# A causal depthwise convolution moved from VectorE to banded products on TensorE, inside the attention stage of a hybrid decoder step

## The chip, the cores and the metric

The kernel runs on one core of one Trainium2 chip. The metric is the device time of one execution, in microseconds; the time shown is the median of three executions.

## The reference, cut to what matters

One inference step of one layer: 2064 prompt rows (16 meta tokens and 2048 tokens) and 8 sample rows with 512 cached positions each. One projection gives the operands of two branches. The convolution branch is a GLU, a causal depthwise convolution of width 31 over 512 channels, a LayerNorm over channels and a swish. The attention branch selects 256 keys a query (128 for the samples) and attends over them.

```python
u = ua * jax.nn.sigmoid(ub)
u_ext = jnp.pad(u, ((0, 0), (CONV_W - 1, 0), (0, 0)))          # samples: 30 rows of state_conv, then u
y = depthwise_conv(u_ext, w) + b                               # [T, 512], width 31
mu = jnp.mean(y, -1); var = jnp.mean((y - mu) ** 2, -1)
cy = silu((y - mu) * rsqrt(var + LN_EPS) * ln_g + ln_b)
o = sparse_attend(q, iq, iw, qpos, k, v, ik, rel_bias, topk)   # 8 heads of 64, 2 kv heads, T5 bias
x = x + concat([cy * silu(gc), o * silu(ga)]) @ w_out
```

## The kernel before, in words

Four functions follow each other, each with one instruction stream per engine and semaphores between them. `project_norm_and_keys` normalises x and makes keys and values. `project_and_select` makes the other projections in chunks of 128 columns by three blocks of up to three tiles of 128 tokens, and between the chunks scores the keys (TensorE and ScalarE) and searches for the selection threshold (VectorE). `attend_and_convolve` does attention and convolution. `mix_out` does the LayerNorm of the convolution, gates, the output projection and the last norm.

`attend_and_convolve` begins with a head: keys are transposed to `kh`, `kl`; 32 pages of K and 32 of V are loaded for the samples (`load_pages`, one DMA each with an address read from a table); the samples' attention runs (`S`, `sS`, then products with `vpage`, line 1387). A table `rrow` of relative biases is computed, written 128 times to DRAM (`d_r`) and read back skewed as `band` and `band16`. GpSimd adds band and mask to `bm`.

Then it takes 65 steps p over `pairs`: step 0 is the 16 rows of the last tile, steps 1 to 64 are the tiles 15 down to 0, four steps a tile, two heads a step. In step p TensorE computes the logits of step p+1 into `psU` (two buffers of 1024 columns, lines 1415 and 1416), VectorE adds mask or band and takes the row maximum (line 1292), ScalarE exponentiates (line 1167), and TensorE transposes the result of step p into `psT` (line 1423), ScalarE copies it to `pts` (line 1136) and TensorE multiplies it with V into `psO` (line 1439). The order on every engine is the program order of its loop; nothing is scheduled at run time.

The convolution is on VectorE: 8 units (4 channel groups by 2 halves of the tokens), each 31 taps of 1088 columns (`conv_tap`, lines 1236 and 1238). `dtaps` spreads these 248 instructions over the steps, behind the eviction of the logits of each step.

SyncE issues nearly all DMAs, in program order, with waits in between (`load_tile`, `load_u`). In `mix_out` the statistics of the LayerNorm are products with a matrix of ones (lines 1823 and 1830), with square, square root, reciprocal and two wide tensor operations per block of four tiles, and the weights are split into a high and a low part in eight pieces (ScalarE line 1663, GpSimd line 1634). TensorE's first product of the output projection (line 1810) waits for all eight.

## Time and profile before

| | |
|---|---|
| median of 3 runs | 2011.85 us (2005.34 to 2012.64) |
| profiled execution | 2016.47 us, its span 2014.5 us |
| busy, share of the span | TensorE 76%, VectorE 70%, ScalarE 36%, GpSimd 19% |
| DMA | 169675 packets, 164.60 MB, queue q1 27.2% of 16 engines |

Rows of the profile give times in microseconds from the start of the span. An engine's idle time in front of an instruction stands in square brackets, with what ended it. PE is TensorE's matmul, PEld its weight load, DVE is VectorE, ACT ScalarE, POOL GpSimd, SPq the issues of SyncE. A matmul on float32 operands makes two records, a transpose or a matmul on float32r operands one.

### The profile page before, as it was taken

Reading aid. Unit: us, or ns where it says so; the run is one execution under the profiler, and the core shown is the slowest. Engines: PE = TensorE matmul, PEld = TensorE weight load, DVE = VectorE, ACT = ScalarE, POOL = GpSimd, SP = SyncE. Lnnn points to the kernel's source line nnn. Section 1 sums busy time; section 2 is a strip of 40 time slices with the busy share of each in tenths; the row PEclk is TensorE's granted clock in tenths of the full one; section 3 lists DMA queues with packets and bytes.
Section 4 is the critical chain, followed back from the end, with each engine's and each line's share of the span. In section 5 each row is a group of like instructions: output and inputs, shape, how many; then the busy total and the mean of one; then the engine's idle time right before and its main releaser. Section 6 shows DMA issues by size and latency. Waiting matters only on the chain. (4 is left out here: it accounts for less than half of the span.)

```text
span 2014.5 us, 26783 instructions
## 1 busy us (share of the span) xinstructions
PE 1529.6 (76%) x9511; PEld 1284.5 (64%) x9511; DVE 1405.1 (70%) x2411; ACT 717.9 (36%) x1255; POOL 379.3 (19%) x265
## 2 busy tenths in 40 slices
PE   5879998399379659692445888888878777359998
PEld 5776997299269659591234666665556555237777
DVE  3414998898888898885018999888789997134442
ACT  3525321322143122221103554555445553254431
POOL 2120432044214114240000000000000112142211
PEclk9989999699689879796657999999899986579999
DMA  7631522023166112221350010111101111522332
GB/s 238 202 87 27 115 79 58 31 75 89 54 215 138 54 52 72 58 68 54 87 128 31 23 53 30 52 46 35 50 27 49 61 47 54 174 90 84 137 140 105
DMA packets 169675, 164.60 MB, mean 82 GB/s; under 512 B 54602, under 2 KB 141618, under 8 KB 169535
## 3 DMA queue, kind: packets, MB, share of 16 engines
q1 hardware_dynamic: 167239, 161.85, 27.2%
q8 instruction: 75, 1.23, 0.3%
q10 hardware_dynamic: 2304, 1.05, 0.2%
q14 instruction: 57, 0.47, 0.1%
HBM read 100.94 MB, written 57.93 MB: 79 GB/s over the span
## 5 line engine op out<-in xcount | busy, mean ns | idle before, releaser
L1238 DVE SCALAR_TENSOR_TENSOR cy<-cu,cw,cy 128x1088 f32<-128x1088 f32 x240 | 345.4, 1439 | 16.3 <-issue 1.3
L645 PE MATMUL psum<-xh,wh 128*128 128x384 f32 (+1 forms) x1056 | 346.4, 328 | 12.4 <-POOL wl L533 10.7
L645 PE MATMUL psum<-xh,wl 128*128 128x384 f32 (+1 forms) x1056 | 345.7, 327 | 0.0
L645 PE MATMUL psum<-xl,wh 128*128 128x384 f32 (+1 forms) x1056 | 345.6, 327 | 0.0
L1136 ACT ACTIVATE pts<-psT 128x512 f32<-128x512 f32 (+1 forms) x302 | 168.5, 573 | 293.3 <-PE psT L1423 282.8
L1415 PE MATMUL psU<-kh,qt 128*128 128x512 f32 (+3 forms) x320 | 139.6, 437 | 98.2 <-DVE mx L1292 96.0
L645 PEld LDWEIGHTS psum<-xh,wh 128*128 128x128 f32 x1056 | 199.0, 188 | 14.1 <-POOL wl L533 10.9
L1439 PE MATMUL psO<-pts,vs 128*64 128x128 f32 x2176 | 187.5, 295 | 23.0 <-ACT pts L1136 22.7
L645 PEld LDWEIGHTS psum<-xl,wh 128*128 128x128 f32 x1056 | 199.2, 189 | 0.0
L645 PEld LDWEIGHTS psum<-xh,wl 128*128 128x128 f32 x1056 | 199.2, 189 | 0.0
L1423 PE MATMUL psT<-cst,L 128*128 128x128 f32 x1105 | 186.8, 303 | 8.7 <-ACT L L1167 8.5
L761 DVE TENSOR_SCALAR_CACHE_REDUCE hit<-scores,T 128x2064 bf16<-128x2064 f32 (+14 forms) x120 | 184.6, 1538 | 11.0
L655 PE MATMUL psum<-ikh,iqs 128*128 128x512 f32 (+4 forms) x172 | 73.0, 427 | 149.3 <-ACT r L610 149.1
L1292 DVE CUSTOM_DVE_ANT_0 L<-psU,mask 128x1024 f32<-128x1024 f32 (+7 forms) x162 | 136.1, 861 | 68.1 <-PE psU L1416 31.1
L1167 ACT ACTIVATE L<-L,nm 128x1920 f32<-128x1920 f32 (+16 forms) x129 | 154.4, 1201 | 72.8 <-DVE nm L1297 72.4
L533 POOL TENSOR_TENSOR wl<-wst,wh 128x1024 fp32r<-128x1024 f32 x44 | 108.3, 2463 | 348.3 <-ACT wh L563 348.3
L1125 POOL TENSOR_TENSOR bm<-band,mask 128x2048 f32<-128x2048 f32 (+1 forms) x16 | 68.0, 4247 | 554.7 <-DMA mask<-d_mask 554.5
L1439 PEld LDWEIGHTS psO<-pts,vs 128*64 128x64 f32 x2176 | 118.7, 141 | 79.6 <-ACT pts L1136 54.2
L1423 PEld LDWEIGHTS psT<-cst,L 128*128 128x128 f32 x1105 | 132.6, 152 | 47.5 <-issue 22.1
L1415 PEld LDWEIGHTS psU<-kh,qt 128*128 128x128 f32 x320 | 67.8, 212 | 130.9 <-DVE mx L1292 95.6
L655 PEld LDWEIGHTS psum<-ikh,iqs 128*128 128x128 f32 x172 | 36.4, 212 | 166.0 <-ACT r L610 160.0
L610 ACT ACTIVATE r<-psum 128x1024 f32<-128x1024 f32 (+6 forms) x100 | 76.8, 807 | 174.5 <-DVE scores L708 143.7
(269 smaller groups left out, 2581.1 us busy)
## 6 DMA issues: line engine op xcount, KB each, us to landing
wst<-in_w_in SPq DMA_DIRECT2D x28, 512.0 KB
wst<-in_w_in SPq DMA_DIRECT2D x32, 256.0 KB
qt<-d_q SPq DMA_DIRECT2D x16, 512.0 KB, 4.2
xst<-in_x_prompt SPq DMA_DIRECT2D x15, 512.0 KB, 3.9
xr<-in_x_prompt SPq DMA_DIRECT2D x15, 512.0 KB, 4.3
out_y_prompt<-fin SPq DMA_DIRECT2D x15, 512.0 KB, 3.0
gate<-d_ga SPq DMA_DIRECT2D x17, 256.0 KB, 4.5
d_mix<-mix SPq DMA_DIRECT2D x17, 256.0 KB, 2.2
```

What stands on the lines that cost most here:

```text
L533: nc.gpsimd.tensor_tensor(out=wl[:, n % 2], in0=wst[:, n % 2], in1=wh[:, n % 2].bitcast(f32), op=ALU.subtract).then_inc(w_lo, 1)
L610: nc.scalar.activation(r[:, m % 2, 0:job[4]], u[:, 0:job[4]], ACT.Relu).then_inc(act_job, 1)
L645: last = nc.tensor.matmul(u[:, 0:k * P], a[:, w % 2, cc, :], x[:, s0:s0 + k, cc, :], start=(cc == 0 and e == 0), stop=(cc == KC - 1 and e ...
L655: nc.tensor.matmul(u[:, b0:b0 + bn], q, mem.ikh[:, a + b0:a + b0 + bn], start=True, stop=False)
L761: V.tensor_scalar(hit[:, 0:width(i)], scores[:, c, 0:width(i)], at[:, c:c + 1] if len(at.shape) == 2 else at[:, c], 0.0, ALU.is_ge, ALU.ad ...
L1136: A.activation(out, src, ACT.Copy).then_inc(act_pt, 1)
L1167: A.activation(L[:, b, 0:width(i)], L[:, b, 0:width(i)], ACT.Exp, bias=nm[:, b:b + 1], accum_out=es[:, tile_no[i] % 2, j % GRP + 4 * side: ...
L1238: V.scalar_tensor_tensor(y, u[:, k:k + HALFW], w, y, ALU.mult, ALU.add)
L1292: last = V.tensor_tensor_reduce(out=L[:, b, x0:x1], in0=U[:, job % 2, x0 - a:x1 - a], in1=in1, scale=1.0, scalar=3 * NEG, op0=ALU.add, op1 ...
L1415: T.matmul(u[:, b0:b0 + bn], q, kh[:, side, a + b0:a + b0 + bn], start=True, stop=False)
L1423: last = T.transpose(pt[:, (side * k + e) * P:(side * k + e + 1) * P], L[:, (2 * p + side) % 4, (b + e) * P:(b + e + 1) * P], ident)
L1439: last = T.matmul(OT[64 * side:64 * side + 64, tile_no[i] % 2, j * P:(j + 1) * P], vs[0:rows, b + e, 64 * side:64 * side + 64], pts[0:rows ...
```

## The change

The depthwise convolution becomes products with banded weight matrices. The tokens are cut into 65 windows of 32 outputs, with 62 input rows each, and 8 more windows hold the samples. For one channel, the weights `ht` are a band of 62 by 32 and the moving operand `uw` is 62 rows by 73 windows, so 512 channels are 512 matmuls, four of them in the four column groups of the array. For that `project_and_select` transposes the GLU output on TensorE (24 jobs `uT`, 68 transposes) and writes it token-major to `d_un`; conv weights go to `d_cw` with zeros around. In attention the channels are taken in four quarters (`load_windows`, `convolve`, `store_conv`), at the ends of steps 1 to 3, 6 to 8, 11 to 13 and 16 to 18. The outputs go to `d_yn` token-major; every second step from 23 on, one tile is loaded as rows, normalised on VectorE (`bn_stats`) and GpSimd (power), transposed by TensorE (`rows_to_columns`) and written to `d_y`. `mix_out` loses the LayerNorm, its weight pieces are split right behind block 0, and the samples' convolution is gone from it.

The head of attention: `rrow` is computed in `project_norm_and_keys` and `d_r` written in `project_and_select`. The page loads are split: SyncE issues 16 of K and 16 of V, GpSimd the others (before, ScalarE issued 16 of K, SyncE the rest). The samples' attention is cut in two on TensorE: the logits of step 0 stand between its scores and its products with V.

```diff
@@ constants
+WIN = 32
+WROWS = WIN + TAPS - 1
+NWP = -(-LP // WIN)
+NW = NWP + NS
@@ project_and_select
+                if name == "ua":
+                    late.append(("uT", h, j, b))
...
+                elif job[0] == "uT":
+                    pe.wait_ge(combined, m + 1)
+                    for e in range(slots(job[1], job[3])[1]):
+                        last = nc.tensor.transpose(u[:, e * P:(e + 1) * P], ust[:, m % 2, e * P:(e + 1) * P], ident)
...
+                if (h, c) == (0, 4):
+                    sp.dma_start(t.d_r.rearrange("t h x -> h t x"), mem.rrow[:, :].unsqueeze(1).to_broadcast([NH, P, BANDX])).then_inc(r_out, 16)
@@ attend_and_convolve
+NQ, QA = 4, 32
+BANKA = 512 // NW
+CONV_JOBS = [(q, a, min(BANKA, QA - a)) for q in range(NQ) for a in range(0, QA, BANKA)]
+CONV_STEPS = [(1, 2, 2, 3, 3), (6, 7, 7, 8, 8), (11, 12, 12, 13, 13), (16, 17, 17, 18, 18)]
+NORM_STEP = [23 + 2 * n for n in range(NT)]
...
+            def load_windows(q):
+                if q:
+                    sp.wait_ge(pe_pt, last_conv(q - 1))
+                else:
+                    sp.wait_ge(uw_zero, 1)
+                for r in range(2):
+                    c0 = 2 * P // 2 * q + 2 * QA * r
+                    at = slice(64 * r, 64 * r + WROWS)
+                    sp.dma_start(ht[at, :, :], bass.AP(t.d_cw.tensor, c0, [[C, WROWS], [C, WIN], [1, 2 * QA]])).then_inc(ht_in, 16)
+                    sp.dma_start(uw[at, 0:NWP, :], bass.AP(t.d_un.tensor, (UROW0 - TAPS + 1) * C + c0,
+                                                           [[C, WROWS], [WIN * C, NWP], [1, 2 * QA]])).then_inc(uw_in, 16)
...
+            def store_conv(q):
+                sp.wait_ge(act_pt, last_conv(q))
+                for g in range(4):
+                    sp.dma_start(bass.AP(t.d_yn.tensor, c0, [[C, WIN], [WIN * C, NWP], [1, QA]]),
+                                 yc[WIN * g:WIN * g + WIN, q % 2, 0:NWP, :]).then_inc(yc_out[q % 2], 16)
...
-            load_pages(sp, range(half), ptab, t.cache_k, "o s n d -> (o s) (n d)", kpage, pg_in)
-            load_pages(sp, range(NS * NPAGE), ptab, t.cache_v, "o s n d -> (o s) (n d)", vpage, vp_in)
+            load_pages(sp, range(hp), ptab, t.cache_k, "o s n d -> (o s) (n d)", kpage, pg_in)
             load_tile(0)
-            sp.wait_ge(rrow_done, 1)
-            sp.dma_start(t.d_r.rearrange("t h x -> h t x"), rrow[:, :].unsqueeze(1).to_broadcast([NH, P, BANDX])).then_inc(r_out, 16)
-            sp.wait_ge(r_out, 16)
...
+            load_pages(sp, range(hp, 2 * hp), ptab, t.cache_v, "o s n d -> (o s) (n d)", vpage, vp_in)
             load_tile(1)
-            load_u(0, dconv, cu[:, 0], cu_in[0])
-            load_u(1, dconv, cu[:, 1], cu_in[1])
+            load_windows(0)
             for p in range(NP_ + 3):
+                for q in range(NQ):
+                    if p == CONV_STEPS[q][-1] + 1:
+                        if q + 1 < NQ:
+                            load_windows(q + 1)
+                        store_conv(q)
...
+            load_pages(pool, range(hp, 2 * hp), ptab, t.cache_k, "o s n d -> (o s) (n d)", kpage, pgp_in)
+            load_pages(pool, range(hp), ptab, t.cache_v, "o s n d -> (o s) (n d)", vpage, vpp_in)
...
-                for tap in range(dtaps[p], dtaps[p + 1]):
-                    conv_tap(tap)
+                for nn in range(NT):
+                    if NORM_STEP[nn] == p:
+                        normalise(nn)
+                    if NORM_STEP[nn] == p + 1:
+                        statistics(nn)
...
+            def statistics(n):
+                dve.wait_ge(yt_in[s], yt_loaded(n))
+                TT(y, y, cbb[:, :], ALU.add)
+                V.bn_stats(st6[:, :], y)
+                V.bn_aggr(mv[:, s, :], st6[:, :]).then_inc(var_done, 1)
...
+            def convolve(e, q, a, k):
+                pt = take_pt(("C", e))
+                if a == 0:
+                    pe.wait_ge(ht_in, 32 * (q + 1))
+                    pe.wait_ge(uw_in, 96 * (q + 1))
+                for x in range(k):
+                    for g in range(4):
+                        r, c = g // 2, QA * (g % 2) + a + x
+                        last = T.matmul(pt[WIN * g:WIN * g + WIN, x * NW:(x + 1) * NW], ht[64 * r:64 * r + WROWS, :, c],
+                                        uw[64 * r:64 * r + WROWS, :, c], start=True, stop=True,
+                                        tile_position=(64 * r, WIN * g))
...
+            def rows_to_columns(n):
+                pe.wait_ge(yn_done, n + 1)
+                for c in range(CC):
+                    last = T.matmul(pt[:, c * P:(c + 1) * P], yt[:, n % 2, c * P:(c + 1) * P],
+                                    flip[:, 1 if TILE_ORDER[n] == LAST else 0, :], start=True, stop=True)
@@ mix_out
-        stages = [(stage, k) for k in range(2) for stage in "abc"]
-        schedule = stages[:5] + [("tile", LAST)] + stages[5:]
+        schedule = [("c", 0), ("tile", LAST), ("c", 1)]
...
-                if w_next < KC:
+                while w_next < KC and (k == 0 or w_next < KC - 2):
                     w_high(w_next)
                     w_next += 1
```

On TensorE's queue, at the end of the samples' attention, the kernel before has this (a row is line, instruction, output and operands, shape and count; `sS` are the samples' probabilities, `q` the queries of step 0):

```order
L1374 MATMUL psU<-bc,relrep 64x1
L1378 MATMUL psT<-cst,sS 128x64 x4
L1381 MATMUL psT<-cst,spick 8x64
L1384 MATMUL psO<-sown,own 128x64
L1387 MATMUL psO<-pts,L 128x8 x32
L1405 MATMUL psU<-kh,q 128x512
```

and the changed kernel has the last piece of those logits (16 columns, which needs the first buffer of `psU` back from VectorE) ahead of the same four groups:

```order
L1537 MATMUL psU<-kh,q 128x16
L1538 MATMUL psU<-kl,q 128x16
L1602 MATMUL psT<-cst,sS 128x64 x4
L1605 MATMUL psT<-cst,spick 8x64
L1609 MATMUL psO<-sown,own 128x64
L1612 MATMUL psO<-pts,L 128x8 x32
L1547 MATMUL psU<-kh,qt 128x512
```

The logits of step 0 have moved in front of the transposes of `sS`.

On SyncE's queue, behind the first tiles of the attention loop, the kernel before has this (a shape is the access pattern of the transfer, outermost count first):

```order
L1038 DMA qt<-d_q 128x1024
L1039 DMA gate<-d_ga 128x4x128
L1041 DMA mask<-d_mask 128x2048
L1046 DMA cu<-d_u 128x1088 x2
L1080 DMA d_mix<-mix 128x512
```

and the changed kernel this:

```order
L1135 DMA qt<-d_q 128x1024
L1136 DMA gate<-d_ga 128x4x128
L1138 DMA mask<-d_mask 128x2048
L1149 DMA ht<-d_cw 62x32x64
L1150 DMA uw<-d_un 62x65x64
L1152 DMA uw<-in_state_conv 30x8x64
L1155 DMA uw<-d_un 1x8x64
L1149 DMA ht<-d_cw 62x32x64
L1150 DMA uw<-d_un 62x65x64
```

The two transfers of 128 rows for the taps have become, for each quarter, four transfers of 62 rows in runs of 64 elements, with the small ones of the samples beside them.

On TensorE's queue the first job of the convolution stands at the end of step 1, between the last products of a step and the logits of the next (`psT` here is the buffer that the transposes use too):

```order
L1555 MATMUL psT<-cst,L 128x128 x4
L1571 MATMUL psO<-pts,vs 64x128 x8
L1584 MATMUL psT<-uw,ht 32x73 x28
L1547 MATMUL psU<-kh,qt 128x512
L1548 MATMUL psU<-kl,qt 128x512
```

Before, the logits of line 1415 stand directly behind the products of line 1439.

## Rows read from the trace of the kernel before

**Rows 1.** By stage: length, busy PE, PEld, DVE, ACT, POOL, clock, DMA share, GB/s.

```profile
152.00:941.30 789.30, 602.56 (x3477) 572.34 (x3475) 659.79 (x1208) 213.10 (x367) 204.94 (x144) 0.89 0.28 76
941.30:1051.70 110.40, 50.64 (x308) 37.42 (x308) 11.72 (x25) 14.32 (x23) 1.35 (x5) 0.64 0.43 102
1051.70:1730.10 678.40, 537.85 (x4117) 395.22 (x4117) 583.62 (x1036) 326.56 (x567) 70.91 (x21) 0.89 0.13 44
1730.10:2014.50 284.40, 229.33 (x912) 173.33 (x912) 104.14 (x87) 104.49 (x161) 68.03 (x44) 0.90 0.38 128
```

**Rows 2.** Groups of instructions and waits, attention loop (1051.7 to 1730.1).

```profile
L1238 DVE SCALAR_TENSOR_TENSOR cy<-cu,cw,cy 128x1088 f32<-128x1088 f32 x240 | 345.4, 1439 | 16.3 <-issue 1.3
L1467 PE MATMUL psT<-cst,rx 128*128 128x128 f32 x128 | 23.1, 336 | 7.9 <-DVE rx L1269 7.9
PE psU L1415 <- DVE mx L1292: 96.0, 42, 15.6
```

**Rows 3.** Timeline of TensorE: early and last steps, and fp32 pitches.

```profile
1074.60 1.65 PE L1423 MATMUL psT<-cst,L 128*128 128x128 f32 x8
1077.60 0.69 PE L1435 MATMUL psO<-pts,vs 128*64 128x64 f32 x16
1078.22 0.66 PE L1423 MATMUL psT<-cst,L 128*128 128x128 f32 x4
1080.56 0.50 PE L1415 MATMUL psU<-kh,qt 128*128 128x512 f32 x1
1122.73 0.50 PE L1415 MATMUL psU<-kh,qt 128*128 128x512 f32 x1
1127.84 1.03 PE L1423 MATMUL psT<-cst,L 128*128 128x128 f32 x8
1137.63 0.50 PE L1415 MATMUL psU<-kh,qt 128*128 128x512 f32 x1
1715.84 0.48 PE L1415 MATMUL psU<-kh,qt 128*128 128x128 f32 x1
1718.56 0.48 PE L1415 MATMUL psU<-kh,qt 128*128 128x128 f32 x1
```

**Rows 4.** Timeline of the head of attention, all engines.

```profile
948.48 17.43 SPq L130 DMA_DIRECT2D L<-in_cache_k  x16
976.95 1.97 PE L1357 MATMUL psT<-cst,L 128*128 128x128 f32 x8 [17.57 <-DMA L<-in_cache_k]
994.37 0.69 DVE L1210 COPY sS<-psU 64x513 f32<-64x513 f32 x1 [34.38 <-PE psU L1374]
1003.61 13.82 PE L1387 MATMUL psO<-pts,L 128*128 128x8 f32 x64
1046.61 0.46 POOL L1123 TENSOR_TENSOR bm<-band,mask 128x144 f32<-128x144 f32 x1 [104.36 <-DMA band<-d_r]
```

**Rows 5.** DMA in 1012 to 1020 (only `d_r` in flight) and in 814 to 819.

```profile
1012.00:1020.00 8.00, 8.00 (x33) 7.42 (x33) 0.81 (x3) 0.00 (x0) 0.00 (x0) 0.50 0.46 52
...
GB/s 0 0 0 0 254 352 270 156 17 25 84 63 86 137 233 266 291 287 287 289 285 287 285 291 272 234 205 162 90 25 12 0 0 0 0 0 0 0 0 0
DMA packets 2224, 0.66 MB, mean 131 GB/s; under 512 B 2096, under 2 KB 2224, under 8 KB 2224
q1 hardware_dynamic: 2224, 0.66, 61.4%
```

**Rows 6.** Output stage: groups of TensorE, last weight piece, first output product.

```profile
L1830 PE MATMUL psS<-tmp,cst 128*128 128x512 f32 (+1 forms) x40 | 19.0, 631 | 24.4 <-ACT tmp L1704 24.4
L1823 PE MATMUL psS<-y,cst 128*128 128x512 f32 (+1 forms) x40 | 18.6, 620 | 6.4 <-DVE y L1740 4.1 <-DMA gc<-d_gc 2.3
1785.31 2.35 POOL L1634 TENSOR_TENSOR wol<-wost,woh 128x1024 fp32r<-128x1024 f32 x1 [4.61 <-ACT woh L1663]
1792.30 1.19 PE L1810 MATMUL psO<-woh,fh 128*128 128x512 f32 x2 [8.73 <-POOL fl L1642]
```

**Rows 7.** Waits of TensorE in the second function (152 to 941).

```profile
PE psum L655 <- ACT r L610: 149.1, 23, 41.3
```

More of the change, by code:

```diff
@@ L90, in constants @@
     at("ones")[:] = 1.0 / C
+    for r in range(128):
+        at("flip")[r, r // WIN * WIN + WIN - 1 - r % WIN] = 1
+    for r in range(WIN):
+        at("flip")[r, 128 + WIN - 1 - r] = 1
+    for r in range(SROW, SROW + NS):
+        at("flip")[r, 128 + r] = 1
     return c
@@ L331, in _ @@
                                                     stop=(c == KC - 1 and k == 2))
+                elif kind == "bias":
+                    pe.wait_ge(bias_in, 32)
+                    last = nc.tensor.matmul(u[0:NH, 0:BANDX], relb[:, :], bcb[:, :], start=True, stop=True)
                 else:
@@ L359, in select_jobs, with put_late @@
 def select_jobs():
-    jobs = []
+    jobs, late = [], []
+    def put_late():
+        jobs.extend(late)
+        late.clear()
     for h, blocks in enumerate(HALVES):
@@ L364, in select_jobs @@
             if (h, c) in SCORE_AT:
+                put_late()
                 g = SCORE_AT[h, c]
@@ L368, in select_jobs @@
                 jobs += [("score", i, head, a, n) for i in GROUPS[g] for head in range(IH) for a, n in pieces(i)]
-            jobs += [("proj", h, c, b) for b in range(len(blocks))]
+            for b in range(len(blocks)):
+                jobs.append(("proj", h, c, b))
+                put_late()
+                if name == "ua":
+                    late.append(("uT", h, j, b))
+    put_late()
     return jobs
@@ L518, in _ @@
             sp.wait_ge(qs_out, 16)
+            sp.wait_ge(r_out, 16)
+            for s in range(2):
+                sp.wait_ge(ut_out[s], 16 * len(ut_jobs[s::2]))
             for k in range(3):
@@ L899, in attend_and_convolve @@
     NP_ = len(pairs)
-    ujobs = [("kT", g, n) for g in range(len(KEYS)) for n in range(NKV)] + [("bias", 0), ("cw", 0), ("S", 0)]
+    ujobs = [("kT", g, n) for g in range(len(KEYS)) for n in range(NKV)] + [("S", 0)]
     for p, (i, j) in enumerate(pairs):
@@ L911, in attend_and_convolve @@
             ptjobs.append(("R", p))
+        ptjobs += [("C", e) for e in range(len(CONV_JOBS)) if CONV_STEP[e] == p]
+        ptjobs += [("Y", n) for n in range(NT) if NORM_STEP[n] == p]
     pt_no = {j: n for n, j in enumerate(ptjobs)}
@@ L917, in attend_and_convolve @@
     band0 = lambda i: max(0, (i - 1) * P)
-    dconv = [(c, h) for h in range(2) for c in range(CC)]
-    def spread(widths, units):
-        total, work = sum(widths[:-2]), len(units) * TAPS
-        return [min(work, -(-work * sum(widths[:n]) // total)) for n in range(len(widths) + 1)]
-    dtaps = spread([width(i) for i, _ in pairs], dconv)
     LW = NT * P
@@ L1126, in band_mask, with inverse_deviation @@
                                 in1=mask[:, s, a:a + k].unsqueeze(1).to_broadcast([128, NH, k]), op=ALU.add).then_inc(bm_ready, 1)
-            for n in range(NT):
-                band_mask(n)
+            def inverse_deviation(n):
+                pool.wait_ge(var_done, n + 1)
+                chained(G.tensor_scalar(ve[:, :], mv[:, n % 2, 1:2], 1.0, LN_EPS, ALU.mult, ALU.add))
+                G.tensor_tensor(out=rs[:, n % 2, :], in0=ve[:, :], in1=mhalf[:, :], op=ALU.pow).then_inc(rs_done, 1)
+            chained(G.memset(mhalf[:, :], -0.5))
+            mask_step = [0, 0] + [first_step(n - 1) + 1 for n in range(2, NT)]
+            for p in range(NP_):
+                for n in range(NT):
+                    if mask_step[n] == p:
+                        band_mask(n)
+                for n in range(NT):
+                    if NORM_STEP[n] == p + 1:
+                        inverse_deviation(n)
         @block.scalar
@@ L1341, in _ @@
             pe.wait_ge(c_in, 32)
-            T.matmul(take_u(("bias", 0))[0:NH, 0:BANDX], rel[:, :], bc[:, 0:BANDX], start=True, stop=True).then_inc(pe_u, 1)
-            pe.wait_ge(cw_in, 16)
-            u = take_u(("cw", 0))
-            for c in range(CC):
-                last = T.transpose(u[:, c * TAPS:(c + 1) * TAPS], cwn[:, c * P:(c + 1) * P], ident[0:TAPS, 0:TAPS])
-            last.then_inc(pe_u, 1)
             pe.wait_ge(s_in, 64)
             T.transpose(take_pt(("own", 0))[:, 0:NS], own[:, 0:128], ident[0:NS, 0:NS]).then_inc(pe_pt, 1)
-            pe.wait_ge(pg_in, 16 * NS * NPAGE)
+            pe.wait_ge(pg_in, 16 * hp)
+            pe.wait_ge(pgp_in, 16 * hp)
             S = take_u(("S", 0))
@@ new lines, in _ @@
+            pt = take_pt(("sT", 0))
+            for g in range(NPAGE):
+                last = T.transpose(pt[:, g * 64:(g + 1) * 64], sS[:, g * P:(g + 1) * P], ident[0:64, 0:64])
+            last.then_inc(pe_pt, 1)
+            pe.wait_ge(spick_done, 1)
+            T.matmul(take_pt(("sP", 0))[0:NS, 0:NS * NH], spick[:, :], ident[0:64, 0:64], start=True, stop=True).then_inc(pe_pt, 1)
+            pe.wait_ge(act_pt, pt_no["sP", 0] + 1)
+            pe.wait_ge(vp_in, 16 * hp)
+            pe.wait_ge(vpp_in, 16 * hp)
@@ new lines, in _ @@
+            T.matmul(OT[:, 0, 0:NS * NH], own[:, 128:256], sown[:, :], start=True, stop=False, skip_group_check=True)
+            for b in range(NS):
+                for g in range(NPAGE):
+                    last = T.matmul(OT[:, 0, b * NH:(b + 1) * NH], vpage[:, b * NPAGE + g, :],
+                                    pts[:, 0, g * 64 + b * NH:g * 64 + (b + 1) * NH], start=False,
+                                    stop=(b == NS - 1 and g == NPAGE - 1), skip_group_check=True)
+            last.then_inc(pe_pv, 1)
@@ L1469, in _ @@
                     last.then_inc(pe_pt, 1)
+                for e, (q, a, k) in enumerate(CONV_JOBS):
+                    if CONV_STEP[e] == p:
+                        convolve(e, q, a, k)
+                for n in range(NT):
+                    if NORM_STEP[n] == p:
+                        rows_to_columns(n)
 WS = 3
```

415 lines of the change are left out of this document (192 added, 223 removed).

## The prediction

> **What bounds the kernel now.** I read the stages first (busy time by stretch), then the waits and groups of the attention loop, then its timeline.
>
> The second function is 789 us long [rows 1], and in it TensorE waits 149.1 us for VectorE's scores, in stretches of up to 41.3 us [rows 7]. VectorE is busy 659.8 of the 789 us there. So VectorE's search sets its end and TensorE has room in each round. The head of attention is 110.4 us with every engine mostly idle. The loop is 678.4 us with VectorE busy 583.6 and TensorE 537.9. The output stage is 284.4 us with TensorE busy 229.3 [rows 1].
>
> In the loop, VectorE's taps are 345.4 us, and TensorE waits 96.0 us, 42 times, for an eviction that stands behind taps [rows 2]. Such waits also lower TensorE's clock: eight transposes behind one took 1.65 us, in a steady step 1.03 [rows 3]. The mean granted clock of the loop is 0.89 of 2.4 GHz [rows 1]. The loop thus has two bounds close together: VectorE in many steps, TensorE in the others.
>
> **The change, part by part.** The sum is made on the span of the profiled execution, 2014.5 us; its own time is 2.0 us more, and the median of the runs is 4.6 below that.
>
> *First two functions.* 68 transposes of the GLU output. Four transposes and what they need take 0.58 us (1078.22 follows 1077.60 by 0.62, a similar group) [rows 3], so some 10 us over all, and each waits for GpSimd's product. They lie before the last scores, under the 149.1 us of [rows 7]: 0. Without that cover they would be 10. One matmul and two small loads in the first function: +1.
>
> *Head.* It now ends with this chain: pages of K, the scores of the samples, softmax, products with V (13.8 us), then the wait for `band`, which GpSimd got only at 1046.6 because `d_r` was written after V's pages and read back [rows 4]. `d_r` is now in DRAM before the head. SyncE issues a page in 1.09 us (17.43 for 16) [rows 4]. SyncE's half of K is issued at 965, its half of V some 13 us later (masks, band, V's table lie between), so at 996. No row shows a page issued by GpSimd; below, nothing over SyncE's 1.09 (its 32 pages done at 979), above I take twice that (1014). K's pages then allow the scores at 968 to 980; scores and softmax take from 977.0 to 994.4 and some 3 more in the trace [rows 4], so they end at 988 to 1000; the logits of step 0 fill the wait for V; their last piece now stands ahead of the samples' products and waits for GpSimd's `bm`, behind its pages. Products with V: 998 to 1012 at the near bound, 1017 to 1031 at the far one. Since the only row of such an issue is SyncE's, I stay near it: the logits of step 1 start at 1012, not 1051.7: **-40** (far bound -20).
>
> *Loop without taps.* I read the starts of all 64 steps (the first logits of each, as 1122.73 and 1137.63, 14.9 us apart, down to 1715.84 and 1718.56, 2.7 apart [rows 3]) and took for each of the 16 tiles the shortest of its four, since these waited least for taps. They are, from tile 15 down, 14.9, 14.4, 13.0, 12.4, 11.6, 10.8, 10.2, 9.5, 8.4, 7.1, 6.2, 5.4, 4.7, 3.5, 3.8 and 2.7 us. Four times the sum is 554; less the last one, which lies in the tail of 11.5, 552; plus the 16 groups of line 1467, which a shortest step lacks, at about 1 us each (128 records in 23.1 [rows 2]), 567; less 4, since step 1 has the short step 0 beside it. That makes 563, where the trace has 667: **-104**. This holds the higher clock too, since the shortest steps run at full clock.
>
> *Convolution on TensorE.* 512 matmuls, 1024 records. The nearest row: 16 records of 64 columns with 64-column weights, one group to the next in 0.62 us, 39 ns each [rows 3]. For 73 columns I take 42: **+43**. Bounds: half of it (21) if the four column groups overlap; 110 if a weight load cannot hide, since 64 records with 8 columns took 13.82 us at half clock, 216 ns each, so 108 at full [rows 4]. The strided operands have no row. 17 times `rows_to_columns`, 8 records each of 128 columns, as line 1467, with one wait of 0.3: **+24**. ScalarE's 37 evictions and VectorE's statistics (some 2 us a tile, in the place of 345 us of taps) lie beside TensorE: 0; they cost only if a tile's rows land late.
>
> *Loads of the windows.* For a quarter there are two transfers of `ht` with 62 by 32 runs and two of `uw` with 62 by 65 runs, all runs of 256 bytes: 12,028 packets. What a packet costs: while a chunk of weights came in runs of 256 bytes, the 16 engines moved at most 291 GB/s, that is 14.1 ns for a packet on one engine; over that window 2224 packets, 2096 of them small, took 61.4% of 16 engines for 5 us, 22 ns each [rows 5]. How many engines work: `d_r`, whose outermost count is 8, was the only transfer in flight from 1012 to 1020, and the DMA share was 0.46, 7.4 engines of 16 [rows 5]. I read this as: a transfer is dealt in equal shares over its outermost count, on as many engines up to 16 as divide it. Of 62, below 16, only 1 and 2 are divisors. Then two engines carry all windows, 6,014 packets each: 6014 x 14.2 ns = 85 us, with some 2 us to land 87. If it were all 16, it would be 11 us.
>
> On this the page "DMA: Bandwidth & Descriptors" of the Trainium skill (section "Why a DMA increments its semaphore by 16 and not by 1") is explicit: the number of engines is the largest one up to 16 that divides the slowest dimension of both access patterns. For 62 rows that is 2 by the page; for 8 rows it is 8, and the trace's 0.46 agrees. By the page alone the sum has the four waits below, by the bare share of 0.46 it could also be without them.
>
> What waits: `convolve` at the end of step 1 stands in TensorE's queue ahead of the logits of step 3, so everything does. Quarter 0 is issued behind SyncE's pages and `load_tile(1)`, at 998, and lands at 1085; TensorE is there at 1012 + 10.4 + 14.9 = 1037 (logits of step 1 in 4.4, step 0's products in 6.0, from 1074.60 to 1080.56 [rows 3], then one step): **+48**. The others are issued when TensorE has done the quarter before, three steps ahead: 44, 39 and 37 us of steps, plus about 1 to issue: **+43, +48, +50**. Each restart at half clock costs about 2 [rows 3]: **+8**. Stores of 128-byte runs (32 rows, so all engines) lie behind and are not waited for.
>
> *Output stage.* The statistics are 37.6 us of records in five blocks. Two blocks come before the first output product; the other three, 24 of 40 records of each line, lie in its steady flow, where TensorE is the bound, and at full clock: **-21** [rows 6]. The first product is at 1792.3, 62.2 us in, behind eight weight pieces that ScalarE interleaves with LayerNorm steps, the last one's low part from 1785.3, after a wait for ScalarE [rows 6]. Without these steps, the first three weights still land as late; behind them I follow GpSimd at 2.35 us a piece, with a wait or two for the next load, to 47 and the first low part of the data to 50: **-12**.
>
> Sum: +1 - 40 - 104 + 43 + 24 + 197 (four waits and the clock) - 33 = **+88**; against the median, 2011.85 + 88 = **2100 us**.
>
> **The rivals.**
>
> *All engines carry the windows (or nearly).* Then 87 us is 11 to 17, below the shortest distance of 37, and nothing waits: 88 - 197 = -109, **1903 us**. For it: the share of 0.46 belongs to one transfer, whose source is also 8 partitions, so it may show the source and not the dealing; 2 engines are read out of 8 by an assumption. Against: 128-row transfers of the same size fill all engines.
>
> *Two engines, but faster.* The sign turns where the four waits sum to 101 us instead of 189: windows in 65 us, 10.5 ns a packet. 14.1 was read with 16 engines at once, two alone might be less held up; or the transfers get different pairs. **1940 to 2008 us**.
>
> *Two engines at the mean price.* With the 22 ns of the whole window, a quarter takes 135 us, each wait grows by 47: **2290 us**. For it: long scattered reads of the same few rows. The write of `d_r` was slower still (52 GB/s over 7.4 engines is 7 bytes a ns, so 36 ns for 256 bytes), which would give 219 us a quarter and **2630**.
>
> *The convolution itself is dear on TensorE.* At 110 instead of 43 the forecast is 2167, and the first rival 1970. Within both, it moves no sign.
>
> **How the numbers follow.** Forecast (two engines near 14 ns) 0.44; all engines 0.20; two but faster 0.08; mean price 0.20; as slow as `d_r` 0.08. The forecast's own range is 2040 to 2230. Cases of both signs hold most of the chance, so the range reaches from 1903 to 2300, with half of the first rival and the dearest one outside. A measurement of this kernel tells about 0.5% from no change. Slower by over 0.5%: 0.70 (forecast less a little, and both dear cases); faster by over 0.5%: 0.27; within: 0.03.
>
> **What would show it.** Right: TensorE waits in front of line 1584 for `uw` or `ht` four times, 40 to 50 us each, in each of which the DMA share is about 0.12 (2 of 16) and all engines are idle; VectorE without taps; `bm` of step 0 before 1000; the first product of line 1810's counterpart about 50 us into the output stage. Wrong: a DMA share near 0.9 for 10 to 20 us behind each `load_windows` and no waits of TensorE. The steps between 19 and 64 tell the rest: they should sum to my shortest steps plus 24.

## The result, and the profile after

| | before | after |
|---|---|---|
| median, runs of one chip | 2008.88 us (2005.34 to 2012.64, 4 runs) | 2203.06 us (2201.03 to 2211.16, 4 runs) |
| span of the profiled execution | 2014.5 us | 2203.1 us |

The changed kernel is slower: 1.0954 times the time before, 95% interval 1.0923 to 1.0985. (The three runs of before that the forecast started from have a fourth beside them here, so their median is 2008.88 and not 2011.85.) I had forecast +88 us and the change is +194. The sign is right, the size is less than half of what came.

The first lines of the page of the changed kernel, to lay beside the table of before:

```profile
span 2203.1 us, 28843 instructions
PE 1530.8 (69%) x10639; PEld 1312.5 (60%) x10639; DVE 1032.1 (47%) x2206; ACT 736.4 (33%) x1297; POOL 406.6 (18%) x331
PE   5979878993794998250299192450887788635998
PEclk9989989997897998675599596685999999867999
DMA packets 263486, 181.56 MB, mean 82 GB/s; under 512 B 137518, under 2 KB 234934, under 8 KB 263340
```

VectorE has lost its taps, 70% to 47%. TensorE is busy as long as before (1530.8 and 1529.6 us), in more time. In the row of slices TensorE has holes (slices 17 to 20 read 2, 5, 0 and 2; a 1, a 2 and a 0 follow), and the granted clock falls with them. The kernel has become one that waits.

By stage (length, busy PE, PEld, DVE, ACT, POOL, clock, DMA share, GB/s), the second function, the head, the attention loop and the output stage, to compare with [rows 1]:

```profile
163.00:930.00 767.00, 604.57 (x3472) 573.73 (x3472) 645.93 (x1208) 216.65 (x381) 211.36 (x143) 0.90 0.31 79
930.00:1103.00 173.00, 50.10 (x302) 37.51 (x303) 11.11 (x26) 14.61 (x24) 23.16 (x38) 0.58 0.31 79
1103.00:1957.00 854.00, 564.73 (x5277) 426.45 (x5277) 262.58 (x856) 351.90 (x602) 73.24 (x53) 0.85 0.19 51
1957.00:2203.00 246.00, 187.97 (x816) 155.05 (x816) 66.50 (x62) 88.12 (x141) 63.00 (x43) 0.87 0.45 145
```

The head went from 110 to 173 us and the loop from 678 to 854, the output stage from 284 to 246. In the loop TensorE is busy only 27 us more than before, yet the loop is 176 us longer.

The head, in the timeline of all engines. SPq rows are issues of SyncE:

```profile
986.39 0.33 SPq L1149 DMA_DIRECT2D ht<-d_cw  x1
986.76 17.07 SPq L1150 DMA_DIRECT2D uw<-d_un  x1
1003.87 30.17 SPq L1152 DMA_DIRECT2D uw<-in_state_conv  x1
...
1080.54 0.43 SPq L1191 DMA_DIRECT2D cbb<-in_conv_b  x1
1083.86 1.22 DVE L1439 CUSTOM_DVE_ANT_0 L<-psU,mask 128x1024 f32<-128x1024 f32 x1 [107.41 <-DMA cbb<-in_conv_b]
...
1085.15 0.38 PE L1537 MATMUL psU<-kh,q 128*128 128x16 f32 x1 [105.04 <-DVE mx L1439]
...
1088.03 13.82 PE L1612 MATMUL psO<-pts,L 128*128 128x8 f32 x64
...
1102.82 0.76 PE L1547 MATMUL psU<-kh,qt 128*128 128x512 f32 x1 [0.98 <-issue]
```

Read it from the end back. The logits of step 1 follow the products with V. These stand in TensorE's queue behind the last piece of step 0's logits, which waits 105 us for a PSUM buffer that VectorE should free. VectorE has not begun: its attention loop opens with a wait for `cbb`, the convolution's bias, and SyncE issues that load only after quarter 0 of the windows. One issue of those windows holds SyncE's queue for 17 us, the next, that of the samples' few rows, for 30. The bias is not needed in step 0 at all; it is first used at step 22.

The loop. The rows are those of windows 1, 2 and 3 and of the tile loads behind them:

```profile
1168.74 0.25 SPq L1149 DMA_DIRECT2D ht<-d_cw  x1
1169.03 13.44 SPq L1150 DMA_DIRECT2D uw<-d_un  x1
1182.51 30.66 SPq L1152 DMA_DIRECT2D uw<-in_state_conv  x1
...
1391.92 2.18 PE L1584 MATMUL psT<-uw,ht 62*32 62x73 f32 x56 [53.26 <-DMA uw<-d_un]
...
1401.36 0.80 PE L1547 MATMUL psU<-kh,qt 128*128 128x512 f32 x1 [7.27 <-DMA qt<-d_q]
1441.60 0.25 SPq L1149 DMA_DIRECT2D ht<-d_cw  x1
...
1530.98 0.62 SPq L1155 DMA_DIRECT2D uw<-d_un  x1
...
1538.45 0.44 SPq L1135 DMA_DIRECT2D qt<-d_q  x1
...
1542.54 0.80 PE L1547 MATMUL psU<-kh,qt 128*128 128x512 f32 x1 [76.43 <-DMA qt<-d_q]
```

The last quarter is issued from 1441.60 to 1531.6, 90 us. TensorE's wait that ends with it is not at `convolve` (L1584). It is at the logits of step 17, for queries of tile 5 that SyncE could issue only at 1538, when the windows and the stores behind them were through. The wait for the windows themselves is hidden in it. The mask of the same tile comes with the queries, and a chain hangs on it: GpSimd makes `bm` from it in 4 us, and VectorE's first eviction waits for that, so TensorE waits 4.3 us once more behind the 76.4:

```profile
1544.42 4.07 POOL L1256 TENSOR_TENSOR bm<-band,mask 128x2048 f32<-128x2048 f32 x1 [137.09 <-DMA mask<-d_mask]
1548.52 1.22 DVE L1439 CUSTOM_DVE_ANT_0 L<-psU,mask 128x1024 f32<-128x1024 f32 x1 [88.56 <-POOL bm L1256]
1549.80 0.80 PE L1547 MATMUL psU<-kh,qt 128*128 128x512 f32 x1 [4.34 <-DVE mx L1439]
```

The two waits in front of L1584 are 49.1 and 53.3 us (102.3 in 2 by the view of waits), that for quarter 0 has gone into the wait for the bias.

While a quarter is under way, the windows view (same columns) shows this; the next two stretches read 0.16 and 0.17:

```profile
1174.00:1184.00 10.00, 9.53 (x100) 6.85 (x98) 1.51 (x7) 4.64 (x8) 0.00 (x0) 1.00 0.17 38
```

34 to 38 GB/s. Two engines with a packet of 256 bytes each 15 ns would move 34 GB/s. The share is a little over 2 of 16 (0.125), so it alone doesn't give the count; the rate fits two, and the experiments tell the rest. By the page "DMA: Bandwidth & Descriptors" of the Trainium skill (section "Why a DMA increments its semaphore by 16 and not by 1"), 62 rows go to 2 engines. The rate of 34 to 38 GB/s agrees.

### The profile page after: what moved, and what is told of

It reads as the page before. It is cut to its first block and busy times, and to the rows that moved or that the text cites. A ratio compares the mean times of both kernels' runs of the same rounds, so it can differ in the third digit from the quotient of the medians.

```text
span 2203.1 us, 28843 instructions
## 1 busy us (share of the span) xinstructions
PE 1530.8 (69%) x10639; PEld 1312.5 (60%) x10639; DVE 1032.1 (47%) x2206; ACT 736.4 (33%) x1297; POOL 406.6 (18%) x331
## 5 line engine op out<-in xcount | busy, mean ns | idle before, releaser
L1547 PE MATMUL psU<-kh,qt 128*128 128x512 f32 (+3 forms) x320 | 134.7, 423 | 128.1 <-DMA qt<-d_q 83.7
L1256 POOL TENSOR_TENSOR bm<-band,mask 128x2048 f32<-128x2048 f32 (+1 forms) x16 | 63.4, 3964 | 819.5 <-DMA mask<-d_mask 819.3
L1571 PE MATMUL psO<-pts,vs 128*64 128x128 f32 x2176 | 181.4, 288 | 26.3 <-ACT pts L1280 26.1
L844 DVE TENSOR_SCALAR_CACHE_REDUCE hit<-scores,T 128x2064 bf16<-128x2064 f32 (+14 forms) x120 | 184.6, 1538 | 11.0
L1555 PE MATMUL psT<-cst,L 128*128 128x128 f32 x1105 | 174.4, 288 | 9.9 <-ACT L L1308 9.8
L1571 PEld LDWEIGHTS psO<-pts,vs 128*64 128x64 f32 x2176 | 113.9, 137 | 81.0 <-ACT pts L1280 56.0
L1555 PEld LDWEIGHTS psT<-cst,L 128*128 128x128 f32 x1105 | 123.2, 144 | 45.3 <-issue 21.1
L1909 PE MATMUL psO<-woh,fh 128*128 128x512 f32 x272 | 85.1, 394 | 54.9 <-POOL fl L1798 54.9
L1548 PE MATMUL psU<-kl,qt 128*128 128x512 f32 (+3 forms) x320 | 121.4, 391 | 0.0
```

The source lines that it names most:

```text
L844: V.tensor_scalar(hit[:, 0:width(i)], scores[:, c, 0:width(i)], at[:, c:c + 1] if len(at.shape) == 2 else at[:, c], 0.0, ALU.is_ge, ALU.ad ...
L1547: T.matmul(u[:, b0:b0 + bn], q, kh[:, side, a + b0:a + b0 + bn], start=True, stop=False)
L1548: last = T.matmul(u[:, b0:b0 + bn], q, kl[:, side, a + b0:a + b0 + bn], start=False, stop=True)
L1555: last = T.transpose(pt[:, (side * k + e) * P:(side * k + e + 1) * P], L[:, (2 * p + side) % 4, (b + e) * P:(b + e + 1) * P], ident)
L1571: last = T.matmul(OT[64 * side:64 * side + 64, tile_no[i] % 2, j * P:(j + 1) * P], vs[0:rows, b + e, 64 * side:64 * side + 64], pts[0:rows ...
L1909: last = T.matmul(O[:, s, h * 512:(h + 1) * 512], a[:, n % FS, c, :], b[:, c, h * 512:(h + 1) * 512], start=(c == 0 and e == 0), stop=(c = ...
```

## The experiments

All ratios are against the kernel before on the same chip. Its median there was 2015.95 us for experiments 1 to 4, 2012.75 for 5 to 8 and 2013.77 for 9.

**1. 64 rows instead of 62** (`rows64`). Window transfers carry two more rows than the products read (the edit is cut here; `d_cw` gets two more rows of zeros).

```
+LROWS = 64
-                    at = slice(64 * r, 64 * r + WROWS)
+                    at = slice(64 * r, 64 * r + LROWS)
-                    ... bass.AP(t.d_cw.tensor, c0, [[C, WROWS], [C, WIN], [1, 2 * QA]])
+                    ... bass.AP(t.d_cw.tensor, c0, [[C, LROWS], [C, WIN], [1, 2 * QA]])
-                    ... [[C, WROWS], [WIN * C, NWP], [1, 2 * QA]]
+                    ... [[C, LROWS], [WIN * C, NWP], [1, 2 * QA]]
```

> The changed kernel, but both window transfers of a half carry 64 rows instead of 62 (two more than the products read; 3% more packets). Theory (a transfer is dealt over the largest divisor of its row count up to 16, so 62 rows go to 2 engines and 64 to 16): a quarter of the windows is in flight 11 to 15 us instead of 90 to 94, DMA share near 0.9 behind each issue, SyncE is hardly held, the waits of TensorE of 49, 53, 7 and 76 us in the loop go, and in the head the bias row is there about 1003 instead of 1084. Time 1900 to 1950 us. Rival (the windows are slow since their short runs read the same few rows of DRAM, whatever the count): unchanged or 3% more per quarter, 2200 to 2215 us.

Measured 1947.45 us (before 2015.95), ratio 0.9653 [0.9625, 0.9682]. One size in two transfers turns 9.5% slower into 3.5% faster. The windows view of the stretch behind the first issue:

```profile
985.00:995.00 10.00, 0.00 (x0) 0.00 (x0) 0.00 (x0) 0.00 (x0) 4.05 (x1) 0.50 0.98 206
```

All engines work, at 206 GB/s where two moved 34. SyncE has issued quarter 0 in 23 us (982.48 to 1005.45) instead of 94, not in the 11 to 15 I expected. VectorE's wait for the bias is 36.9 us instead of 107.4, and of the loop's waits of 49, 53, 7 and 76 us only 10.3 us for queries at step 17 are left (and 4.2 behind them). The time is in the range that I expected. The rival, that the scattered reads are slow whatever their count, is out.

**2. 63 rows** (`rows63`). The same edit with 63.

> The changed kernel with 63 rows in the window transfers. Theory of the divisor: 63 has the divisor 9, so nine engines with 1358 packets each at 15.5 ns, 21 us a quarter, DMA share 0.56 meanwhile; total within 5 to 15 us above the kernel with 64 rows, since only the head waits for a quarter. Rival (only powers of two, or even counts, spread well; 63 odd goes to 1 engine): 190 us a quarter, 2500 us or more. Rival (the row count is nothing): 2203 us.

Measured 1957.89 us, ratio 0.9707 [0.9686, 0.9728], 10 us above 64 rows. The same view:

```profile
988.00:998.00 10.00, 0.00 (x0) 0.00 (x0) 0.00 (x0) 0.00 (x0) 4.05 (x1) 0.50 0.63 163
```

The share is 0.63 here and 0.51 in the ten microseconds behind it, about 9 of 16 (0.56). So one more row, an odd count, goes from two engines to nine: the largest divisor fits all three counts, and neither evenness nor a power of two does. SyncE is held 27.7 us (985.50 to 1013.19), where I expected 21.

**3. The bias ahead of the windows** (`cbb_first`). The loads of `flip` and `cbb` move up; windows have 62 rows.

```
+            sp.dma_start(flip...).then_inc(flip_in, 16)
+            sp.dma_start(cbb[:, :], ...).then_inc(cb_in, 16)
             load_windows(0)
-            sp.dma_start(flip...).then_inc(flip_in, 16)
-            sp.dma_start(cbb[:, :], ...).then_inc(cb_in, 16)
```

> The changed kernel with the loads of the flip matrices and of the convolution's bias put ahead of the first quarter's windows in SyncE's queue. Theory (VectorE waits for the bias before its whole loop, and that is what holds the head to 1085; behind it only the windows' own wait stays, which hides steps 1 and 2): VectorE's wait of 107 us goes to under 5, logits of step 1 start at 1015 to 1025 instead of 1103, TensorE then waits some 40 to 50 us in front of the convolution for the windows, and 30 to 45 us are saved: 2160 to 2175 us. Rival (the head is held by the windows' transfer itself, since pages of V or tiles share its engines): logits of step 1 still after 1080 and 0 to 10 us saved.

Measured 2158.81 us, ratio 1.0699 [1.0675, 1.0724]. Against the changed kernel, on another chip, that is 44.6 us less by the spans, 44.3 by the medians and 51 by the ratios. From the timelines of VectorE and TensorE:

```profile
989.26 1.22 DVE L1439 CUSTOM_DVE_ANT_0 L<-psU,mask 128x1024 f32<-128x1024 f32 x1 [15.60 <-DMA cbb<-in_conv_b]
```
```profile
1008.22 0.76 PE L1547 MATMUL psU<-kh,qt 128*128 128x512 f32 x1 [0.98 <-issue]
```
```profile
1082.95 1.34 PE L1584 MATMUL psT<-uw,ht 62*32 62x73 f32 x32 [48.28 <-DMA uw<-d_un]
```

The logits of step 1 start at 1008.2, and TensorE waits 48.3 us for quarter 0 at L1584. My forecast had 1012 and 48. This kernel is near the one that I had in mind when I worked out the head; the changed kernel has a wait of 91 us more. But the agreement is in part luck. VectorE still waits 15.6 us for the bias here (I expected under 5), since SyncE's pages of V and `load_tile(1)` are ahead of it, and TensorE 14.2 us for VectorE. Counted from its own start the head is 81.8 us long (926.4 to 1008.2), where the forecast has 70; the second function ended 15 us earlier than before and hides that.

**4. The kernel before without taps** (`before_no_taps`). Only the first of the 31 taps of each unit is left, so the convolution is not computed.

```
+                elif k < TAPS - 1:
+                    return
-                else:
-                    V.scalar_tensor_tensor(y, u[:, k:k + HALFW], w, y, ALU.mult, ALU.add)
```

> The kernel before, in which VectorE does only the first of the 31 taps of each unit; the loads and stores of the convolution stay. It leaves the other taps out, so the convolution is not computed. My term: the loop goes from 667 to 563 us, so 104 us less, 1905 us. Rival (the shortest step of a tile is a lucky one, or other waits step in, as GpSimd's statistics or masks): 50 to 80 us less, 1930 to 1960.

Measured 1902.87 us, ratio 0.9434 [0.9396, 0.9473]. In its trace step 1 starts at 1053.21 and step 64 at 1613.69: 560.5 us, where before has 666.9 (1051.65 to 1718.56). I had 563 from the shortest step of each tile. The term of -104 is -106 in the loop. The whole kernel takes 113 us less, since the stretch behind step 64 falls too, from 295.9 to 288.7.

**5. Tile 5 ahead of the last windows** (`tile_first_2`), on top of 3.

```
+                if p == 14:
+                    sp.wait_ge(tile_done, 4)
+                    load_tile(5)
                 for q in range(NQ):
                     if p == CONV_STEPS[q][-1] + 1: ...
```

> The kernel with the bias loaded first (2158.8 us), and the loads of tile 5 put ahead of the last quarter's windows in SyncE's queue, all else the same. Theory (SyncE's queue stands still while it issues the windows, so a tile's load behind them is issued some 90 us late): TensorE's wait of 76 us for the queries at step 17 goes; in its place comes the windows' own wait in front of the convolution in step 16, 48 to 54 us, as I had it in the forecast. 20 to 28 us saved: 2131 to 2139 us. Rival (the 76 us are the windows' wait with some late restart, the order of the issue is nothing): 2155 to 2162 us.

Measured 2131.33 us, ratio 1.0590 [1.0554, 1.0626] to a before of 2012.75; against experiment 3, on another chip, that is 22 us less by the ratios, 27.5 by the medians and 29.3 by the spans. TensorE's timeline:

```profile
1486.03 1.21 PE L1587 MATMUL psT<-uw,ht 62*32 62x73 f32 x28 [54.34 <-DMA uw<-d_un]
```

The wait of 76 us for queries has gone and the windows' own wait of 54.3 us stands at `convolve`, where I had forecast 50. Steps 16 and 17 together take 82.0 us instead of 110.9. These 29 us are the price of a load in line behind a blocked issue: 22 of waiting, and 7 for what follows it, 4.5 of them TensorE's wait for VectorE and so for the late mask. The time is in the range that I expected.

**6. Tiles issued by ScalarE** (`tiles_by_scalar_2`), on top of 3. `load_tile(3)`, `(4)` and `(5)` stand in ScalarE's program behind the exponentials of steps 7, 11 and 15; same transfers, same waits.

> The kernel with the bias loaded first, and the loads of tiles 3, 4 and 5 issued by ScalarE instead of SyncE, at the point where VectorE has released the buffers, while the windows are under way on SyncE's queue. Theory (only the issue is blocked; the two busy DMA engines share themselves between queues): queries land within some 10 us, the waits of 7 and 76 us for them go, the windows wait of step 16 of 48 to 54 us shows; 27 to 35 us saved in all, 2124 to 2132 us. Rival (a load that is issued meanwhile stands behind the windows' packets on the two DMA engines that carry them, since 128 rows use all sixteen): the queries still land only with the windows, and nothing or up to 10 us is saved.

Measured 2131.77 us, ratio 1.0577 [1.0538, 1.0616]. ScalarE's issues of a tile in the timeline, and the line of the DMA view with size and median time to landing:

```profile
1167.79 0.34 ACTq L1317 DMA_DIRECT2D qt<-d_q  x1
1168.16 0.45 ACTq L1318 DMA_DIRECT2D gate<-d_ga  x1
...
qt<-d_q ACTq DMA_DIRECT2D x3, 512.0 KB, 8.0
```

ScalarE issues in 0.3 to 1.3 us while SyncE stands, and its queries land in 8.0 us at the median (4.2 in the changed kernel, where the windows are through by then). No wait for queries is left. The windows come later: quarters 1 to 3 are waited for 52.3, 57.2 and 58.3 us, against 49.3, 53.6 and 54.3 in experiment 5. So a transfer that another queue sends gets through, and it is SyncE's queue that is held. That the windows come later because the tile's packets take a share of the two busy engines fits these numbers; no view shows which engine carries what.

**7. 64 rows and the bias first** (`rows64_cbb_2`), 1 and 3 together.

> Windows with 64 rows (1947.5 us) and the bias and the flip matrices loaded ahead of the first windows. Theory: the wait of 34 us for VectorE in the head goes, logits of step 1 start near 1008 as with the bias first alone, and the windows, landed by about 1008, are not waited for in step 1: 18 to 24 us saved, 1923 to 1930 us. Rival (the pages of V from GpSimd end no earlier than the bias did): 0 to 8 us.

Measured 1933.32 us, ratio 0.9596 [0.9562, 0.9630]. Against experiment 1, on another chip, the ratio falls by 0.006, some 11 us, and the span by 13; I expected 18 to 24. Step 1 starts at 1012.9 instead of 1028.4, which is 15.5 us, and quarter 0 is not waited for. TensorE's wait for VectorE in the head falls from 34.3 to 14.9 us, the bias still being what VectorE waits for, and the head itself from 102.2 to 82.9, which is 19.3 us. The second function, which the edit doesn't touch, ended 3.7 us later in this profile than in that of experiment 1 (930.0 and 926.3).

**8. And the inverse deviation ahead of the mask** (`rows64_cbb_inv_2`).

```
                 for n in range(NT):
+                    if NORM_STEP[n] == p + 1:
+                        inverse_deviation(n)
+                for n in range(NT):
                     if mask_step[n] == p:
                         band_mask(n)
-                for n in range(NT):
-                    if NORM_STEP[n] == p + 1:
-                        inverse_deviation(n)
```

> As the kernel with 64 rows and the bias first, and in GpSimd's loop the inverse deviation of a tile stands ahead of the mask of the next tile instead of behind it. Theory (the long steps 28, 32, 36 to 52 come from VectorE's normalisation, which waits for GpSimd, which waits for a mask's transfer): these steps fall from 9 to 17 us to those of the kernel without taps plus 1.5, VectorE's waits of 74 us in 9 go to under 10, and 20 to 30 us are saved beside the kernel without this edit: 1897 to 1907 us. Rival (the rows themselves or ScalarE's eviction are late): 0 to 8 us.

Measured 1899.85 us, ratio 0.9437 [0.9402, 0.9472], 33.5 us less than experiment 7 on the same chip, more than the 20 to 30 that I expected. What it takes away is best seen in the changed kernel: GpSimd's timeline around step 48, then VectorE's line there.

```profile
1870.85 4.05 POOL L1256 TENSOR_TENSOR bm<-band,mask 128x2048 f32<-128x2048 f32 x1 [19.56 <-DMA mask<-d_mask]
1874.99 0.19 POOL L1261 TENSOR_SCALAR ve<-mv 128x1 f32<-128x1 f32 x1
1875.26 0.55 POOL L1262 TENSOR_TENSOR rs<-ve,mhalf 128x1 f32<-128x1 f32 x1
```
```profile
1875.85 0.55 DVE L1389 TENSOR_SCALAR uw<-uw,mv,rs 128x512 f32<-128x512 f32 x1 [10.63 <-POOL rs L1262]
```

A power of 128 numbers, 0.55 us, stands on GpSimd behind a mask that has not landed. VectorE waits for it, and TensorE for VectorE. The view of waits of the changed kernel has it in one line, and that of experiment 8 has none like it any more:

```profile
DVE uw L1389 <- POOL rs L1262: 73.9, 9, 11.1
```

Step 48 is 11.6 us in the changed kernel, 5.6 here, and 4.7 without taps and rows. From the start of step 19 to that of step 64 it is 365.4 us in the changed kernel, 340.4 here and 310.0 in experiment 4.

**9. All four edits** (`rows64_all`), 8 with the edit of 5.

> The kernel with 64 rows, the bias first and the inverse deviation first (1899.9 us), and the loads of tile 5 ahead of the last quarter's windows. Theory (SyncE is held some 25 us by the windows even with sixteen engines, and the wait of 9 us for the queries at step 17, with 4 us behind it, comes from that): both waits go, the windows themselves are not waited for, and 8 to 13 us are saved: 1887 to 1892 us. Rival (the queries' own transfer is slow beside the windows, or the windows then come late for step 16): 0 to 4 us: 1896 to 1900 us.

Measured 1879.95 us (6 runs; before 2013.77, 11 runs), ratio 0.9348 [0.9320, 0.9375]. Both waits at step 17 are gone: steps 16 and 17 take 12.3 and 15.3 us, not 21.4 and 21.5. That is 15.3 us; the medians, on two chips, differ by 19.9, which is more than I expected. The spans of the two profiled executions differ by 30.8 us, since that of experiment 9 is the fastest of its six runs: besides the 15.3, the second function ends 5.2 us earlier, steps 19 to 63 are 6.5 us shorter and what lies behind step 64 is 4.1 us shorter. Why, no run shows. This version beats both kernels: 6.5% less time than before, 14.7% less than the changed one.

## Why the prediction was right or wrong

The spans, place by place. The loop is read from the start of step 1's logits to that of step 64's, the rest behind it is the tail and the output stage.

| | forecast | measured | read from |
|---|---|---|---|
| first two functions | +1 | -11 | second function ends at 930.5, not 941.3 |
| head, with what quarter 0 costs behind it | -40 +48 = +8 | +62 | 172.4 instead of 110.4; no wait behind it |
| taps out of the loop | -104 | -106 | experiment 4, 560.5 |
| convolution and other waits in steps 1 to 18 | +43 | +41 | 477.7, less 250.5 in experiment 4, less the 186.1 of the next row |
| waits for windows and for tiles behind them | +43 +48 +50 = +141 | +186 | 49.1, 53.3, 7.3 and 76.4 |
| rows back to columns, steps 19 to 63 | +24 | +55 | 365.4, less 310.0 in experiment 4 |
| clock behind the waits | +8 | in the rows above | about 8, see below |
| tail and output stage | -33 | -39 | 257.2 instead of 295.9 |
| sum | +88 | +189 | |

**Right.** The sign, and for the reason given: TensorE waits for windows. That the windows are dealt to two engines, and what a packet costs: 85 us forecast for 6,014 packets, 94 measured in the head and 90 in the last quarter (15.6 and 15.0 ns; forecast 14.2). The price of the convolution: 56 records take 2.18 us, 39 ns each, where I took 42, so the strided operands show no cost, a weight load of 32 columns hides, and no overlap of the four column groups shows. The first output product 50.1 us into its stage (2007.59), forecast 50. GpSimd issues a page each 1.14 us, close to SyncE's 1.09, the near bound that I chose.

**Right in part by luck.** The +41 beside +43 holds more than the convolution. In experiment 1 steps 1 to 18 take 293.4 us, and less its 10.3 and the 250.5 of experiment 4 that is 32.6. So the restarts behind the changed kernel's waits cost some 8.5 us more than there (forecast +8), and the 32.6 are some 41 of convolution and a step 1 that is 8.6 us shorter than in experiment 4 (11.8 and 20.4). For the taps, the number is right and its working has a slip. The list of shortest steps has 8.4, which is a step of the tile whose shortest is 7.1, and lacks the 3.9 of the last tile but one. Read rightly, the sixteen give 545 us and a term of -122. The loop without taps took 560.5, as the first step of a tile is longer than its shortest and step 1 alone takes 20.4. The two errors nearly cancel.

**Wrong, first: quarter 0.** The step that failed is "What waits", with "`convolve` at the end of step 1 stands in TensorE's queue ahead of the logits of step 3, so everything does" and +48 there. I asked which instruction reads the windows and not what else stands behind them in SyncE's queue. `cbb` does, and VectorE waits for it ahead of its whole loop. So what I had saved in the head (-40) did not come, and neither the samples' products with V nor steps 1 and 2 (some 26 us) were there to hide the load. It cost 54 us on a span: +62 instead of +8. In experiment 3, with two lines moved, the head is 28.6 us shorter than before and quarter 0 is waited for 48.3 us, which makes +20. So 42 of the 54 us are the order of the bias and the windows. The other 12 are the head itself, which I had 12 us too short: in experiment 3 TensorE still waits 14.2 us there for VectorE, and so for the bias.

**Wrong, second: SyncE's queue.** The same paragraph says that the stores "lie behind and are not waited for", and does not speak of tiles. It gives a quarter about 1 us to be issued. In fact an issue of `uw` holds the queue 13 to 31 us, until nearly all of the quarter is through, and with it `load_tile`. That makes 7.3 and 76.4 us out of one wait of 50, and 186 out of 141. Experiments 5 and 6 show the cause from two sides: earlier in the same queue, or in another queue, and the wait is gone.

**Wrong, third: rows to columns.** I costed it as matmuls and one wait of 0.3 us each. The chain is SyncE's load of the rows, VectorE's statistics, GpSimd's power, VectorE's normalisation, TensorE. I put VectorE's part beside TensorE ("0; they cost only if a tile's rows land late") and did not look at GpSimd's order, in which the power stands behind a band mask. The term was 24 and the measured one 55; 25 of the 31 us between go with experiment 8. The 30 us left are near the 24.

**Of the rivals**, "all engines carry the windows" was worked out as 1903 us. The kernels with 64 rows realise it: 1947 with the bias and GpSimd's order as they are, 1900 with both moved. That 1900 meets 1903 is in part luck too: the second function ended 11 us earlier and the head was 12 us too long for it, and these nearly cancel. "Two engines, but faster" (10.5 ns a packet), as slow as `d_r` (36 ns) and "Two engines at the mean price" (22 ns, 2290 us) are refuted by 15 to 15.6 ns a packet, though the time measured, 2203, lies a little nearer to 2290 than to the forecast. The time was no evidence for either; the rows were. The dear convolution (110 us) is refuted by 39 ns a record.

**The second function** ended 10.9 us earlier, which I did not foresee and tried no experiment on. It ended at 941.3 and 942.1 us in the two kernels without the change and between 924.6 and 932.7 in the nine with it. VectorE sets its end and was busy 14 us less there. Part of it is one small group of 40 instructions, first before, then after:

```profile
L771 DVE COPY_PREDICATED hi<-lt,T 128x6 f32<-128x6 int32 x40 | 16.3, 407 | 0.0
```
```profile
L854 DVE COPY_PREDICATED hi<-lt,T 128x6 f32<-128x6 int32 x40 | 6.5, 162 | 0.0
```

Before, 29 of them overlap no GpSimd instruction and take 0.17 us. Eleven do: five that start some 40 ns behind a GpSimd instruction last until it ends (1.00 us once, 2.38 to 2.39 four times), and six that start before it or within 60 ns of its end take 0.16. After, seven overlap one, all in the second way, and take 0.16. The Trainium skill, page "SBUF — State Buffer", section "Who interferes with whom", says that a VectorE instruction with two inputs in SBUF contends with a GpSimd instruction that reads SBUF, and that the order of issue decides which of the two is kept out. The rows of both kernels agree with it: none starts in the midst of a GpSimd instruction and is short. These 9.8 us are most of the 14. That the added transposes moved GpSimd's work in time, and so the collisions, is argued and not shown. Nor is it shown that the function ends earlier for it: in experiment 4 the same group took only 11.8 us, 4.5 less than before, and the function ended at 942.1 and no earlier.

## What to carry to other kernels

Give a DMA's outermost count a large divisor up to 16, if need be by carrying rows that nobody reads: 62, 63 and 64 rows made 2203, 1958 and 1947 us of one kernel. Before costing a slow transfer, list what stands behind it in its issuer's queue and which engine waits for each of these at the head of a loop; here the transfer's own four waits (48, 49, 53 and 54 us in experiments 3 and 5) were forecast within 7 us each, and the things behind it were the larger error. And where a small result is made on an engine that also waits for transfers, put it ahead of that wait: moving a power of 0.55 us and the small step ahead of it was worth 33 us (experiment 8).

## What the runs showed of the hardware

- An issue on SyncE's queue is not short when the DMA engines it uses are behind. With two engines one issue of `uw` took 13.3 to 17.1 us and the one behind it 30.0 to 30.7; with sixteen 2.0 to 4.7 and 5.8 to 8.1. A quarter has nearly as many packets in both (12,028 and 12,416), so their number does not set it. ScalarE's issues, made while SyncE was held, took 0.3 to 1.3 us.
- Packets of 256 bytes got dearer with the number of engines on these overlapping windows. For quarter 0, from SyncE's first issue to its release: 15.6 ns a packet and engine with 2 (93.7 us, 6,014 packets), 20.4 with 9 (27.7 us, 1,358), 29.6 with 16 (23.0 us, 776). From 9 to 16 engines a quarter gained only 4.7 us. Why, no run here shows.
- VectorE's small selections on 6 columns took 0.16 us, but 1.00 to 2.39 us in the five cases in which they started some 40 ns behind a GpSimd tensor-tensor instruction; these ended with it. An overlap in which they started first, or at the other's end, cost nothing.
